# Second block's end to latents: three strips of a projection tile by tile, high parts first, and squares summed with tokens on the partitions

## What is computed

```python
def rms_norm(x, g):
    y = x * lax.rsqrt(jnp.mean(x * x, axis=-1, keepdims=True) + EPS)
    return y * g

# layer 0 of the second block ends, layer 1 begins
h = h + rms_norm(y, post_norm[0])            # y = mix @ w_out of the even layer
u = rms_norm(h, pre_norm[1])
cq, ckv, k_rope, gate = split_cols(u @ w_in, (384, 256, 64, 1024))
q  = rms_norm(cq,  q_a_norm)  @ w_qb         # 8 heads x (128 + 64)
kv = rms_norm(ckv, kv_a_norm) @ w_kvb        # 8 heads x (128 + 128)
# rope on 64 columns of q and on k_rope, causal attention, gate, @ odd_w_out
```

## Time and profile before

| | |
|---|---|
| median of 3 runs | 1934.63 us |
| lowest, highest | 1931.15, 1936.31 us |
| the profiled execution | 1931.33 us |
| its span, first to last instruction | 1929.5 us |
| mean granted TensorE clock | 0.971 |
| busy: PE, DVE, ACT, POOL | 96%, 46%, 39%, 46% |

### The profile page before, as it was taken

The page is one execution under the profiler, slowest core; times in us unless marked ns, Lnnn a source line. Parts: engine busy times, 40 slices in busy tenths (PEclk is TensorE's granted clock), DMA queues, the critical chain, the costliest instruction groups (busy, mean ns, idle before and its releaser), DMA issues.

```text
span 1929.5 us, 24996 instructions
## 1 busy us (share of the span) xinstructions
PE 1857.0 (96%) x8846; PEld 1518.8 (79%) x8846; DVE 887.8 (46%) x1298; ACT 748.6 (39%) x1172; POOL 883.3 (46%) x1178
## 2 busy tenths in 40 slices
PE   4889999999999999999999999999999999899997
PEld 3777888888888767888888888788888878687776
DVE  8994232121225699532121225751255551466653
ACT  5533343231324568533232324523232332333662
POOL 1015545555555621555554545564554455262222
PEclk8579999999999999999999999999999999999999
DMA  4134332323332321222323323352322323131111
GB/s 162 44 99 137 98 97 93 104 88 98 98 98 88 108 80 39 86 89 98 99 98 98 98 91 95 89 158 91 94 77 77 88 78 97 60 120 55 34 55 44
DMA packets 51458, 173.63 MB, mean 90 GB/s; under 512 B 6704, under 2 KB 7088, under 8 KB 50736
## 3 DMA queue, kind: packets, MB, share of 16 engines
q1 hardware_dynamic: 49952, 169.62, 28.6%
q10 hardware_dynamic: 1424, 2.88, 0.5%
HBM read 161.27 MB, written 2.10 MB: 85 GB/s over the span
## 4 chain that ended last, share of the span: by engine, by line
PE 35%; issue 29%; POOL 27%; DVE 7%; ACT 1%; POOLq 0%; DMA 0%; SPq 0%; ACTq 0%; DVEq 0%
POOL wlo L491 27%; PE ps L929 10%; PE ps L931 9%; PE ps L930 9%; PE ps L1362 1%; PE ps L1353 1%; PE ps L1352 1%; PE ps L1115 1%; DVE E L334 1%; DVE E L329 1%; PE ps L1082 0%; PE ps L1000 0%; DVE bt L330 0%; PE ps L995 0%; DVE zz L1490 0%
## 5 line engine op out<-in xcount | busy, mean ns | idle before, releaser
L491 POOL TENSOR_TENSOR wlo<-raw,whi 128x256 fp32r<-128x256 f32 x1152 | 867.4, 789 | 997.0 <-ACT whi L531 964.7
L531 ACT ACTIVATE whi<-raw 128x1024 fp32r<-128x1024 f32 x288 | 302.0, 1052 | 374.9 <-PE ps L931 368.2
L929 PE MATMUL ps<-Ch,whi 128*128 128x512 f32 x912 | 361.7, 397 | 0.5 <-POOL wlo L491 0.5
L931 PE MATMUL ps<-Ch,wlo 128*128 128x512 f32 x912 | 355.4, 390 | 0.0
L930 PE MATMUL ps<-Cl,whi 128*128 128x512 f32 x912 | 355.0, 389 | 0.0
L929 PE MATMUL ps<-Ah,whi 128*128 128x512 f32 x656 | 264.5, 403 | 6.1 <-DVE Al L1590 4.3
L931 PE MATMUL ps<-Ah,wlo 128*128 128x512 f32 x656 | 256.2, 391 | 0.0
L930 PE MATMUL ps<-Al,whi 128*128 128x512 f32 x656 | 255.9, 390 | 0.0
L929 PE MATMUL ps<-Bh,whi 128*128 128x512 f32 x640 | 250.2, 391 | 0.0
L931 PE MATMUL ps<-Bh,wlo 128*128 128x512 f32 x640 | 249.0, 389 | 0.0
L930 PE MATMUL ps<-Bl,whi 128*128 128x512 f32 x640 | 249.0, 389 | 0.0
(11 more groups left out here) (365 smaller groups left out, 2096.4 us busy)
## 6 DMA issues: line engine op xcount, KB each, us to landing
raw<-in_w SPq DMA_DIRECT2D x288, 512.0 KB, 3.6
u<-in_xch SPq DMA_DIRECT2D x1, 2048.0 KB, 8.8
vsw<-vsb SPq DMA_DIRECT2D x16, 128.0 KB, 2.3
zsw<-zz SPq DMA_DIRECT2D x16, 128.0 KB, 2.3
h<-in_xfm SPq DMA_DIRECT2D x2, 1024.0 KB, 6.5
out<-h SPq DMA_DIRECT2D x8, 256.0 KB, 2.1
bB<-in_bc SPq DMA_DIRECT2D x1, 1024.0 KB, 10.8
bC<-in_bc SPq DMA_DIRECT2D x1, 1024.0 KB, 14.4
```

Source lines behind the costliest of these rows:

```text
L491: last = nc.gpsimd.tensor_tensor(wlo[:, r, cc], raw[:, r, cc], whi[:, r, cc].bitcast(F32), ALU.subtract)
L531: nc.scalar.activation(whi[:, slot, :], raw[:, slot, :], ACT.Copy).then_inc(hi_ready, 1)
L929: nc.tensor.matmul(out, whi[:, slot, w], xh, start=first, stop=False)
L931: return nc.tensor.matmul(out, wlo[:, slot, w], xh, start=False, stop=last)
```

## The change

1. **Three strips tile by tile.** A new `odd_strips` takes the place of `first_strips("odd", 2, ...)`. For each tile it multiplies the high part of the input with the high and the low weights of all three strips (six matmuls), waits for the low part, and adds the three products of high weights with it.
2. **DVE's loop** no longer runs a whole tile ahead: behind the addition of tile m comes the scaled y of tile m + 1, then the low part of tile m.
3. **Squares.** `add_squares` uses the squares as the weights and one column of ones as the moving operand: four matmuls of 128x1 (each two passes) into bank SZ in place of one of 128x512.
4. **The factor.** The root and the reciprocal go over 128x4 numbers. TensorE spreads them (`token_factors`) behind the third tile of strip 3, into bank SY, and ACT copies that to `rstd`. ACT splits the next strip between the root and this copy.
5. The swap of the rotary keys moves from behind strip 2 to behind strip 3. The counts of `nrm_bc` and `tok_rc` follow.

```diff
--- before.py
+++ after.py
@@ -270,6 +270,7 @@
         in_a1, in_rt, in_cm = sem("in_a1"), sem("in_rt"), sem("in_cm")
         fin, out_sem = sem("fin"), sem("out_sem")
         fin_low, scaled_y, rstd_sb, pool_mul = sem("fin_low"), sem("scaled_y"), sem("rstd_sb"), sem("pool_mul")
+        odd_rstd = sem("odd_rstd")
 
         tabs, ang, sq_x, ss_x, ss_ps, std_x, u_ready = (sem(n) for n in ("tabs", "ang", "sq_x", "ss_x", "ss_ps", "std_x", "u_ready"))
         c_ready = sem("c_ready")
@@ -864,10 +865,16 @@
                 if m >= 2:
                     act.wait_ge(sq_used, m - 1)
                 nc.scalar.activation(squares[m % 2][:, :], h[:, m, :], ACT.Square).then_inc(sq_made, 1)
-            root(D)
+            nrm[0] += 1
+            act.wait_ge(nrm_ps, nrm[0])
+            nc.scalar.activation(tok_std, ps[:, SZ, 0:NB], ACT.Sqrt, bias=eps, scale=1.0 / D).then_inc(nrm_std, 1)
+            ahead("odd", 1)
+            act.wait_ge(nrm_bc, 2)
+            nc.scalar.copy(rstd[:, :], ps[:, SY, :]).then_inc(odd_rstd, 1)
             O0 = OUT0["odd"]
             for m in range(5):
-                ahead("odd", 1 + m)
+                if m:
+                    ahead("odd", 1 + m)
                 act.wait_ge(evac, O0 + 1 + m + 1)
                 high("L", m, kn[:, m, :], gain("qa", m) if m < 3 else gain("kva", m - 3))
                 answer(nc.scalar.activation(ev[:, 0, :] if m == 4 else sq[:, :], kn[:, m, :], ACT.Square))
@@ -913,7 +920,7 @@
             act.wait_ge(evac, OUT0["oout"] + KT)
             for m in range(DVE_TILES, KT):
                 nc.scalar.activation(ybuf3[:, m, :], ybuf3[:, m, :], ACT.Copy, scale=gain("post1", m)).then_inc(scaled_y, 1)
-            act.wait_ge(nrm_bc, 3)
+            act.wait_ge(nrm_bc, 4)
             nc.scalar.copy(rstd[:, :], ps[:, SX, :]).then_inc(rstd_sb, 1)
             assert xs[0] == XT["oo"] + 8
 
@@ -1058,10 +1065,33 @@
                 if part == 3:
                     last.then_inc(seg_done, 1)
 
+            def token_sums(x, first, last):
+                for j in range(NB):
+                    done = nc.tensor.matmul(ps[:, SZ, j:j + 1], x[:, j * P:(j + 1) * P], C("ones")[:, 0:1], start=first and j == 0, stop=last and j == NB - 1)
+                return done
+
             def add_squares(k):
                 pe.wait_ge(sq_made, k + 1)
-                last = nc.tensor.matmul(ps[:, NRM, :], C("ones"), squares[k % 2][:, :], start=(k == 0), stop=(k == KT - 1))
-                last.then_inc(sq_used if k < KT - 1 else nrm_ps, 1)
+                token_sums(squares[k % 2], k == 0, k == KT - 1).then_inc(sq_used if k < KT - 1 else nrm_ps, 1)
+
+            def odd_strips():
+
+                pe.wait_ge(lo_ready, S0["odd"] + 3)
+                pe.wait_ge(evac, OUT0["odd"] + 3 - RING)
+                for k in range(KT):
+                    w = slice(k * P, (k + 1) * P)
+                    xh, xl = X["A"][0][:, k, :], X["A"][1][:, k, :]
+                    at = [((S0["odd"] + l) % RING, ps[:, (OUT0["odd"] + l) % RING, :]) for l in range(3)]
+                    pe.wait_ge(x_hi, XT["odd"] + k + 1)
+                    for slot, out in at:
+                        nc.tensor.matmul(out, whi[:, slot, w], xh, start=(k == 0), stop=False)
+                        nc.tensor.matmul(out, wlo[:, slot, w], xh, start=False, stop=False)
+                    pe.wait_ge(x_lo, XT["odd"] + k + 1)
+                    for slot, out in at:
+                        last = nc.tensor.matmul(out, whi[:, slot, w], xl, start=False, stop=(k == KT - 1))
+                        if k == KT - 1:
+                            last.then_inc(seg_done, 1)
+                    add_squares(k)
 
             def strips(name, x, xt, step=1, n=8, between=None):
 
@@ -1089,23 +1119,21 @@
                         strips(f"down{layer}_{c}", HIDDEN[layer][c % 2], XT[f"hid{layer}_{c}"])
                 strips(f"gate{layer}", "B", XT[f"gate{layer}"], between=norm)
 
+            def token_factors(n, banks):
+                pe.wait_ge(tok_rc, n)
+                for bank in banks:
+                    for j in range(NB):
+                        last = nc.tensor.matmul(ps[:, bank, j * P:(j + 1) * P], tok_rstd[:, j:j + 1].to_broadcast([P, P]), C("ident"), start=True, stop=True)
+                    last.then_inc(nrm_bc, 1)
+
             def token_norm(i):
-
-                def token_sums(x, first, last):
-                    for j in range(NB):
-                        done = nc.tensor.matmul(ps[:, SZ, j:j + 1], x[:, j * P:(j + 1) * P], C("ones")[:, 0:1], start=first and j == 0, stop=last and j == NB - 1)
-                    return done
 
                 nrm[0] += 1
                 pe.wait_ge(ssq_ready, nrm[0])
                 token_sums(acc, True, False)
                 pe.wait_ge(last_sq, i + 1)
                 token_sums(sq, False, True).then_inc(nrm_ps, 1)
-                pe.wait_ge(tok_rc, i + 1)
-                for bank in (SY, SX)[:i + 1]:
-                    for j in range(NB):
-                        last = nc.tensor.matmul(ps[:, bank, j * P:(j + 1) * P], tok_rstd[:, j:j + 1].to_broadcast([P, P]), C("ident"), start=True, stop=True)
-                    last.then_inc(nrm_bc, 1)
+                token_factors(2 * i + 1, (SY, SX)[:i + 1])
 
             def partners(src, bank, perm="perm2"):
                 nc.tensor.matmul(ps[:, bank, :], C(perm), src, start=True, stop=True).then_inc(rope_ps, 1)
@@ -1318,10 +1346,14 @@
                     last.then_inc(seg_done, 1)
             token_norm(0)
 
-            first_strips("odd", 2, "A", XT["odd"], each=add_squares)
-            for l in range(2, NSTR["odd"]):
-                strip("odd", l, l, "A", XT["odd"])
-                if l == 2:
+            def factors_behind(k):
+                if k == 2:
+                    token_factors(2, (SY,))
+
+            odd_strips()
+            for l in range(3, NSTR["odd"]):
+                strip("odd", l, l, "A", XT["odd"], each=factors_behind if l == 3 else None)
+                if l == 3:
                     pe.wait_ge(evac, OUT0["odd"] + 1)
                     partners(kr, SX)
             norm()
@@ -1945,21 +1977,27 @@
                 nrm[0] += 1
                 dve.wait_ge(nrm_std, nrm[0])
                 V.reciprocal(tok_rstd, tok_std).then_inc(tok_rc, 1)
-                dve.wait_ge(nrm_bc, norms[0])
+                dve.wait_ge(nrm_bc, 2 * norms[0] - 1)
                 dve.wait_ge(evac, OUT0[name] + KT)
 
             post("eout", ybuf, 2)
-            for m in range(KT + 1):
-                if m < KT:
-                    if m >= 2:
-                        dve.wait_ge(to_act, asks[0] - 1)
-                    ch.link(V.scalar_tensor_tensor(ev[:, m % 2, :], ybuf[:, m, :], gain("post0", m), ps[:, SY, :], ALU.mult, ALU.mult))
-                    ask(V.tensor_tensor(h[:, m, :], h[:, m, :], ev[:, m % 2, :], ALU.add))
-                if m:
-                    dve.wait_ge(to_act, asks[0] - (m < KT))
-                    low("A", m - 1, h[:, m - 1, :], gain("pre1", m - 1))
-
-            root()
+            def block_output(m):
+                if m >= 2:
+                    dve.wait_ge(to_act, asks[0] - 1)
+                ch.link(V.scalar_tensor_tensor(ev[:, m % 2, :], ybuf[:, m, :], gain("post0", m), ps[:, SY, :], ALU.mult, ALU.mult))
+
+            block_output(0)
+            for m in range(KT):
+                ask(V.tensor_tensor(h[:, m, :], h[:, m, :], ev[:, m % 2, :], ALU.add))
+                if m + 1 < KT:
+                    block_output(m + 1)
+                dve.wait_ge(to_act, asks[0])
+                low("A", m, h[:, m, :], gain("pre1", m))
+
+            nrm[0] += 1
+            dve.wait_ge(nrm_std, nrm[0])
+            V.reciprocal(tok_rstd, tok_std).then_inc(tok_rc, 1)
+            dve.wait_ge(odd_rstd, 1)
             scaled("odd", 0, kr)
             start_sum()
             for m in range(5):
```

## The result

| | before | after |
|---|---|---|
| median of 9 runs | 1933.80 us | 1938.32 us |
| lowest, highest | 1931.15, 1936.31 | 1935.96, 1941.11 |
| the profiled execution | 1931.33 | 1936.47 |
| its span | 1929.5 | 1934.4 |

The median lies inside the range of 1931.5 to 1941.5.

What follows compares the result with a forecast made beforehand. TensorE bounds from 1664.5 us to the last projection's end; 1.8 us gained at the start, 0.1 + 0.2 + 0.9 lost to pitch, sums and broadcast, 0.2 rounding, 3.1 new waits: 2.7 slower, median 1937.3, range 1931.5 to 1941.5.

Steps and rivals of the forecast that it cites:

- Start: First product on TensorE follows the high part instead of the low part, at 1662.7, a gain of 1.8 us.
- Low clock: Half-rate clock at the first tile still costs 1.6 us, as before; bounds 0.8 to 2.5.
- Sums: Eight groups of one-column matmuls at 0.90 us replace sums of 0.87: +0.2 us, no gain in TensorE time.
- rival of nearly free sums: Small sums' loads hide under products, a group costs 0.23 us: 2.7 us faster, 1931.9; chance 0.08.
- First scaling: DVE starts scaling the first output at 1692.0 instead of 1688.3, 3.7 us later.
- The two new waits: TensorE waits 1.6 us at the sum over the query latents and 1.5 us at the fifth query output.
- The fifth output: TensorE starts the fifth query output at 1718.4 instead of 1715.77, 2.7 us later.
- some 2.05 us a tile: DVE's need per tile when nobody holds it; TensorE needs 3, so later tiles wait for nobody.
- distance of 3.3 us between the profiled execution and the median: Median of three runs lies 3.3 us above the profiled execution; carried over to forecast the median after.
- The total: Whole kernel 2.7 us slower, median 1937.3 us; forecast given 0.60.

Runs made afterwards that it cites:

- e4: The changed kernel with the old 128x512 square sums, three strips and high parts first kept: +4.0 us against the kernel before.
- e1: The changed kernel with the rotary-key rotation moved from the second latent tile to behind the fifth to seventh query outputs: +0.8 us against the kernel before.
- e7: The kernel before with one unused 128x512 reciprocal added on DVE in the latent chain: +4.7 us against the kernel before.
- e9: The changed kernel with one-pass 128x512 square sums in the fast format, rotation in its old place: -2.0 us against the kernel before.
- e6: Two strips, high parts first, fast-format square sums and late rotary-key rotation: -3.3 us against the kernel before.
- e10: The changed kernel with TensorE waiting in each tile for the low part before the first product: +5.0 us against the kernel before.
- e8: The changed kernel with two strips in the block instead of three, new sums kept: +1.5 us against the kernel before.
- e11: A repeat of the changed kernel with two strips instead of three, new sums kept: +3.1 us against the kernel before.

## Why the prediction was right

- **Start.** First product forecast at 1662.7; 1663.98 - 1.17 = 1662.8. Right.
- **Low clock.** 1.6 us of loss kept. The profile has the same 6.8 us at half clock as before. Right for this execution; other kernels had longer stretches (last section).
- **Sums.** A group of one-column matmuls was to cost 0.90 us in the stream, a tile 2.98: measured 1671.99 - 0.23 - 1670.87 = 0.89, and 2.97. e4 shows what follows from it with three strips, that exchanging the sums does nothing. The rival of nearly free sums is out: eight records with a load each take 0.95 us with one column and 1.05 with 128 (L1070 and L1126 above), so the loads set the pace. The Trainium skill's section on the issue gap ("TensorE: Matmul & The Clock Gate") had pointed to that rival. The section on LDWEIGHTS of the same page of the Trainium skill gives a load P/1.2 ns, an estimate of 107 ns for 128 columns or 0.85 us for eight, and the 0.89 agrees with it.
- **First scaling.** Forecast 1692.0; 1693.39 - 1.17 = 1692.2. Right.
- **The two new waits.** Forecast 1.6 and 1.5; 1.37 and 1.43. Their cause, the chain of DVE and ACT that lost the strip it hid behind, is shown by e1, e7 and e9: with the chain shortened both waits go, with it lengthened the second appears in the old kernel too.
- **The fifth output.** Forecast 2.7 later, measured 3.15. About 0.2 us of the difference is there at the first scaling, 0.1 of it from the start, and about 0.3 comes in the latent chain: 1719.99 - 1693.39 = 26.6 us from the first scaling until the first query output has left its bank, where I had taken over 26.3 from the kernel before.
- **What was mis-sized.** DVE's need of "some 2.05 us a tile" was read from the old order. In the new one the low part stands 0.23 us behind ACT's cast of the same tile, and a tile takes 2.24. In the change TensorE needs 2.97, so it cost nothing; with cheap sums it is the next bound (e6). The distance of 3.3 us between the profiled execution and the median was also no constant: with nine runs it was 2.5.
- **The total.** +2.7 against +4.5 (2.3 to 5.6). The block accounts for 3.15; the rest was not in the prediction, and that the median lies in the range owes something to a range 10 us wide. Longer stretches at half clock do not explain the rest: the mean granted clock of the nine runs is 0.9697, that of the 85 runs of the kernel before in the experiments 0.9694. The median of the spans is 1935.3 us against 1931.7 in those 85, 3.6 longer. The rest lies outside the span: the device time exceeds it by at most 1.9 us in the kernel before, by 1.9 to 2.1 in seven of these nine runs, and by 3.0 in two, one of them the median run. What takes this time is not known.

## What to carry to other kernels

Before work is moved forward because it can start early, look at what ran beside it: a strip that comes sooner may have been the cover of a reciprocal and of a chain on two other engines, and its slack (here 1.0 to 1.2 us) is the limit of the gain. A sum by matmul is bought by its passes and its weight loads, so turning it round with one column saves nothing when eight loads replace two long passes; the fast format does save, at the price of precision, once the next bound is lifted too. When a table of waits names an engine, check when that engine was done: five kernels here (the change, e4, e7, e9, e10) have GpSimd named for the wait at the fifth query output, and in the change its splits were done 3.8 us before.

## What the runs showed that was not expected

The low stretch at the block's beginning lasted 6.8, 10.2 or 13.6 us in thirteen profiled executions. In the eight kernels with old or fast sums it was 6.8 seven times and 10.2 once; in the five with one-column sums it was 6.8, 10.2, 10.2, 13.6 and 13.6. This suggests that a block with a share of one-column matmuls is granted the full clock later, at a cost of 1.7 or 3.4 us, and it would account for the blocks of e8 and e11. It is not shown: each profile is one execution, and the blocks that began latest (from 1658.85 us on, in one kernel with the old sums too) are also those with the long stretches. Over all runs the difference is smaller: the mean granted clock of the whole span is 0.9691 in the 53 runs of the kernels with one-column sums and 0.9695 in the 69 of the other experiments, 0.8 us of some 1934, and in the changed kernel itself it is not below the kernel before.

The late beginnings are themselves in good part the clock's. e1's block begins 5.75 us later than that of the kernel before, though the order ahead of it is the same; ahead of it the missing clock, summed as above, is 54.6 us in that execution and 47.8 in the kernel before. So a few microseconds between two executions can stand where neither kernel differs, which is why places are read here from the block's first matmul.

The time outside the span differs too. In 12 of the 53 runs of the kernels with one-column sums (e1 has five of them) the device time exceeds the span by 2.8 to 3.8 us; in none of the other runs is it more than 2.3. No run here shows why.
